# A gated decoder block on one core: features squared by partition quarters, turned in one operation, and two more feed-forward pairs by seven products

## The reference

```python
    hn = rms_norm(x, norm_mlp[l]).astype(dt)
    x = x + jnp.square(jax.nn.relu(hn @ w_up[l])) @ w_down[l]
```

## Time and profile before

| | us |
|---|---|
| median of 3 runs | 1327.31 (1327.13 to 1327.4) |
| the profiled execution | 1326.47 |
| its span, first to last instruction | 1324.7 |
| PE busy | 1320.1 |
| DVE busy | 1097.0 |
| ACT busy | 701.4 |

### The profile page before, as it was taken

One profiled execution on the slowest core, in us unless ns is written; L12 is line 12 of the kernel. 1 busy time (PEld: TensorE's weight loads), 2 busy tenths in 40 slices (PEclk: granted clock), 3 DMA queues, 4 the chain that ended last, 5 costly groups with the idle time before them and its releaser, 6 DMA issues.

```text
span 1324.7 us, 15784 instructions
## 1 busy us (share of the span) xinstructions
PE 1320.1 (100%) x5962; PEld 1095.4 (83%) x5962; DVE 1097.0 (83%) x1554; ACT 701.4 (53%) x889; POOL 16.6 (1%) x31
## 2 busy tenths in 40 slices
PE   9999999999999999999999999999999999999999
PEld 8988888888888888888888888788888888888887
DVE  6788699777477875999889998999866899899986
ACT  6656554566545444354555554555535555555553
POOL 0101000000000000000000000000000000000000
PEclk9999999999999999999999999999999999999999
DMA  9656555555556666464666665565676666556563
GB/s 319 206 177 216 195 190 179 191 181 169 186 163 203 242 215 191 166 220 162 222 190 191 192 192 190 182 213 183 216 221 189 192 191 193 191 168 211 194 218 128
DMA packets 115173, 259.57 MB, mean 196 GB/s; under 512 B 4334, under 2 KB 7452, under 8 KB 114844
## 3 DMA queue, kind: packets, MB, share of 16 engines
q1 hardware_dynamic: 115068, 258.57, 59.6%
q10 hardware_dynamic: 32, 0.01, 0.0%
HBM read 256.46 MB, written 2.10 MB: 195 GB/s over the span
## 4 chain that ended last, share of the span: by engine, by line
PE 96%; DVE 3%; issue 0%; ACT 0%; DVEq 0%; ACTq 0%
PE ps L1237 23%; PE ps L1239 23%; PE ps L1238 23%; PE ps L1247 7%; PE ps L1248 7%; PE ps L1249 7%; DVE w_lo L1109 2%; DVE ps L795 1%; PE ps L1392 1%; PE ps L1373 1%; PE ps L1341 1%; PE ps L1337 1%; PE ps L1339 1%; PE ps L1347 0%; ACT w_hi L716 0%
## 5 line engine op out<-in xcount | busy, mean ns | idle before, releaser
L477 ACT ACTIVATE w_hi<-raw 128x1024 fp32r<-128x1024 f32 (+1 forms) x349 | 368.0, 1061 | 379.7 <-PE ps L1239 363.8
L777 DVE TENSOR_TENSOR w_lo<-raw,w_hi 128x1024 fp32r<-128x1024 f32 (+1 forms) x349 | 423.9, 1222 | 166.5 <-ACT w_hi L477 163.4
L1237 PE MATMUL ps<-w_hi,xT 128*128 128x512 f32 x1088 | 425.7, 391 | 0.0
L1239 PE MATMUL ps<-w_hi,xT 128*128 128x512 f32 x1088 | 423.5, 389 | 0.0
L1238 PE MATMUL ps<-w_lo,xT 128*128 128x512 f32 x1088 | 423.3, 389 | 0.0
L1239 PEld LDWEIGHTS ps<-w_hi,xT 128*128 128x128 f32 x1088 | 204.2, 188 | 42.8
L1237 PEld LDWEIGHTS ps<-w_hi,xT 128*128 128x128 f32 x1088 | 204.3, 188 | 41.9
L1238 PEld LDWEIGHTS ps<-w_lo,xT 128*128 128x128 f32 x1088 | 204.3, 188 | 41.8
L716 ACT ACTIVATE w_hi<-raw 128x1024 fp32r<-128x1024 f32 (+1 forms) x152 | 147.7, 991 | 97.9 <-PE ps L1249 80.1
L1109 DVE TENSOR_TENSOR w_lo<-raw,w_hi 128x1024 fp32r<-128x1024 f32 (+1 forms) x152 | 167.9, 1137 | 24.3 <-ACT w_hi L716 22.4
L795 DVE STREAM_TRANSPOSE ps<-gate 32x256 f32<-32x256 f32 x272 | 124.0, 456 | 4.9
(11 more groups left out here) (242 smaller groups left out, 1360.8 us busy)
## 6 DMA issues: line engine op xcount, KB each, us to landing
raw<-in_w_in_dram SPq DMA_DIRECT2D x73, 1024.0 KB, 5.1
raw<-in_w_up_dram SPq DMA_DIRECT2D x64, 1024.0 KB, 5.3
raw<-in_w_down_dram SPq DMA_DIRECT2D x64, 1024.0 KB, 5.1
raw<-in_w_out_dram SPq DMA_DIRECT2D x16, 1024.0 KB, 5.2
raw<-in_w_branch_b_dram SPq DMA_DIRECT2D x8, 1024.0 KB, 5.3
raw<-in_w_branch_a_dram SPq DMA_DIRECT2D x8, 1024.0 KB, 5.1
raw<-in_w_in_dram SPq DMA_DIRECT2D x4, 1040.0 KB, 9.7
rows<-in_x_dram SPq DMA_DIRECT2D x1, 2048.0 KB, 9.9
```

The lines of the kernel that those rows point to most:

```text
L477: act.activation(dst[:, k % RING, :, :], src[:, k // 2, KH * (k % 2):KH * (k % 2) + KH, :], ACT.Copy).then_inc(hi_made, 1)
L777: dve.tensor_tensor(lo[:, k % RING, :, :], src[:, k // 2, KH * (k % 2):KH * (k % 2) + KH, :], hi[:, k % RING, :, :].bitcast(F32), ALU.subt ...
L1237: pe.matmul(o, hi, w_hi[:, s, i, :], start=first, stop=False)
L1239: last = pe.matmul(o, lo, w_hi[:, s, i, :], start=False, stop=end)
```

## The change

In each of the 16 up blocks ScalarE squares in 16 instructions of 32 partitions x 256 elements, four in each of the slots 1 to 4, and each writes its 32 partitions to the partition band into which it is to be turned. VectorE then turns the whole 128x1024 in one instruction in slot 5, in place of sixteen.

In the last half (f = 1, n = 1) the pairs 14 and 15 also go by seven products, which makes eight of them. The order there becomes 0, 3, 1, 5, 2, 7, 4, 9, 11, 6, 13, 8, 14, 15, 10, 12: 9 and 11, and 14 and 15, now follow directly on each other, and the last two are the whole pairs 10 and 12. For the two new pairs VectorE makes sums of features in f = 1 in slot 75 (five operations of 128x256 out of PSUM), ScalarE copies their hi part in slot 76 (128x1024), and VectorE subtracts in slot 77 (128x1024). They lie where `xT` lay, which the last up step has read by then.

```diff
-ORDER = ((0, 1, 2, 4, 6, 3, 5, 8, 7, 10, 9, 11, 12, 13, 14, 15), (0, 3, 1, 5, 2, 7, 4, 9, 6, 11, 8, 13, 10, 12, 14, 15))
-PARTS = [[4 if i in SEVEN else 2 for i in ORDER[n]] for n in range(2)]
+LATE = (14, 15)
+ORDER = (((0, 1, 2, 4, 6, 3, 5, 8, 7, 10, 9, 11, 12, 13, 14, 15), (0, 3, 1, 5, 2, 7, 4, 9, 6, 11, 8, 13, 10, 12, 14, 15)),
+         ((0, 1, 2, 4, 6, 3, 5, 8, 7, 10, 9, 11, 12, 13, 14, 15), (0, 3, 1, 5, 2, 7, 4, 9, 11, 6, 13, 8, 14, 15, 10, 12)))
+PARTS = [[[4 if i in SEVEN or f == n == 1 and i in LATE else 2 for i in ORDER[f][n]] for n in range(2)] for f in range(2)]
...
+        with nc.sbuf_tensor("late_f", [P, 4 * S], F32) as late_f, nc.sbuf_tensor("late_ops", [P, 2, 4, 2, P], F32R) as late_ops:
+            pass
         xT = sb("xT", [P, KT, 2, S], F32R)
...
# ScalarE, up_jobs
-                if j < 8 and at == 1:
-                    act.wait_ge(up_read, 8 * f + j + 1)
-                    act.activation(up_sq, up_pos, ACT.Square).then_inc(up_squared, 1)
+                if j < 8 and 1 <= at < 5:
+                    if at == 1:
+                        act.wait_ge(up_read, 8 * f + j + 1)
+                    r = P // 4 * (at - 1)
+                    read = up_pos.rearrange("p (m t q c) -> p q m t c", m=M, t=4, q=4)
+                    moved = up_sq.rearrange("p (m q t c) -> p q m t c", m=M, t=4, q=4)
+                    for q in range(4):
+                        last = act.activation(moved[32 * q:32 * q + 32, r // 32, :, :, :], read[r:r + 32, q, :, :, :],
+                                              ACT.Square)
+                    if at == 4:
+                        last.then_inc(up_squared, 1)
...
+                if f == 1 and i == 76:
+                    act.wait_ge(pair_sum, 2 * len(SEVEN) + 1)
+                    act.activation(late_parts[:, :, 0, :], late_rows, ACT.Copy).then_inc(pair_hi, 1)
...
# VectorE, up_jobs
-                if j < 8 and 2 <= at < 6:
-                    if at == 2:
-                        dve.wait_ge(up_squared, 8 * f + j + 1)
-                    turn_blocks(turned, squared, 4 * at - 8, 4 * at - 4, up_turned if at == 5 else None)
+                if j < 8 and at == 5:
+                    dve.wait_ge(up_squared, 8 * f + j + 1)
+                    dve.transpose(turned.rearrange("p (t b c) -> p b t c", t=4, c=32),
+                                  up_sq.rearrange("p (b t c) -> p b t c", t=4, c=32)).then_inc(up_turned, 1)
...
+                if f == 1 and i == 75:
+                    a11, a21, a12, a22 = (ps[:, 2 * u:2 * u + 2, P * c:P * c + P] for c in range(4))
+                    dve.wait_ge(w_used, 8 * (B_UP + FB + 8))
+                    link(dve.tensor_copy(late_4, a21))
+                    dve.tensor_tensor(late_3, a11, late_4, ALU.subtract)
+                    link(dve.tensor_tensor(late_1, late_4, a22, ALU.add))
+                    link(dve.tensor_tensor(late_2, late_1, a11, ALU.subtract))
+                    dve.tensor_tensor(late_4, a12, late_2, ALU.subtract).then_inc(pair_sum, 1)
+                if f == 1 and i == 77:
+                    dve.wait_ge(pair_hi, 2 * len(SEVEN) + 1)
+                    dve.tensor_tensor(late_parts[:, :, 1, :], late_rows, late_parts[:, :, 0, :].bitcast(F32),
+                                      ALU.subtract).then_inc(pair_lo, 1)
...
# TensorE, seven_pair
-                s1, ops = a21, sum_ops(i)
+                ops = sum_ops(i)
+                s1 = ops[:, 3, :, :] if i in LATE else a21
...
                 if first and n == 0:
                     pe.wait_ge(up_lo_made, 8 * f + 8)
+                    if f == 1:
+                        pe.wait_ge(pair_sum, 2 * len(SEVEN) + 1)
```

More of the change, by code:

```diff
@@ L155, in build @@
         e_t = gate_f[:, 0:768].rearrange("p (b c) -> p b c", b=2)
+        late_k = late_f[:, :].rearrange("p (b k c) -> p b k c", b=2, k=4)
+        late_1, late_2, late_3, late_4 = (late_k[:, :, k, :] for k in (3, 0, 1, 2))
+        late_rows = late_f[:, :].rearrange("p (r c) -> p r c", c=P)
+        late_parts = late_ops[:, :, :, :, :].rearrange("p b k a c -> p (b k) a c")
         up_pos = gate_f[:, 0:1024]
@@ L277, in step_of, with last_shared @@
         def step_of(f, n, at, part=0):
-            return 8 * (B_UP + FB * f + 8) + (sum(PARTS[0]) if n else 0) + sum(PARTS[n][:at]) + part
+            return 8 * (B_UP + FB * f + 8) + (sum(PARTS[f][0]) if n else 0) + sum(PARTS[f][n][:at]) + part
         def place_of(f, s):
-            n = 0 if s < sum(PARTS[0]) else 1
-            s -= n * sum(PARTS[0])
+            n = 0 if s < sum(PARTS[f][0]) else 1
+            s -= n * sum(PARTS[f][0])
             at = 0
-            while s >= PARTS[n][at]:
-                s -= PARTS[n][at]
+            while s >= PARTS[f][n][at]:
+                s -= PARTS[f][n][at]
                 at += 1
             return n, at, s
-        def last_shared(n):
-            return max(at for at in range(16) if PARTS[n][at] == 4)
+        def last_shared(f, n):
+            return max(at for at in range(16) if PARTS[f][n][at] == 4)
         def sum_ops(i):
+            if i in LATE:
+                return late_ops[:, LATE.index(i), :, :, :]
             q = SEVEN.index(i)
@@ L300, in diffs_before @@
         def diffs_before(f, n, at):
-            return 2 * (len(SEVEN) * (2 * f + n) + sum(x == 4 for x in PARTS[n][:at]))
+            return 2 * (len(SEVEN) * (2 * f + n) + sum(x == 4 for x in PARTS[f][n][:at]))
         def gate_kept(n):
@@ L392, in _ @@
                 for n in range(2):
-                    for at, i in enumerate(ORDER[n]):
+                    for at, i in enumerate(ORDER[f][n]):
                         k = at % RAW
@@ L1109, in down_lo @@
                 dve.tensor_tensor(lo, src, hi.bitcast(F32), ALU.subtract).then_inc(lo_made, 1)
-                if PARTS[n][at] == 4 and part == 1:
+                if PARTS[f][n][at] == 4 and part == 1:
                     quarters = raw[:, k, :, :]
@@ L1119, in first_sums @@
                 diffs = w_diff.rearrange("p (a n) -> p a n", n=N)
-                before = [step_of(f, n, x, 2) for x in range(at) if PARTS[n][x] == 4]
+                before = [step_of(f, n, x, 2) for x in range(at) if PARTS[f][n][x] == 4]
                 dve.wait_ge(landed[at % RAW], 16 * (B_UP + 16 * f + 8 + 4 * n + at // RAW) + 16)
@@ L1203, in _ @@
                 blk0 = B_UP + FB * f
-                for i in range(12, 64 + DOWN + (12 if f == 0 else 0)):
+                for i in range(12, 64 + DOWN[f] + (12 if f == 0 else 0)):
                     up_jobs(f, i)
@@ L1207, in _ @@
                         split_lo(blk0 + i // 8, i % 8)
-                    elif i < 64 + DOWN:
+                    elif i < 64 + DOWN[f]:
                         n, at, part = place_of(f, i - 64)
-                        if part == PARTS[n][at] - 1 and at < 15 and PARTS[n][at + 1] == 4:
+                        if part == PARTS[f][n][at] - 1 and at < 15 and PARTS[f][n][at + 1] == 4:
                             first_sums(f, n, at + 1)
@@ L1213, in _ @@
                     else:
-                        split_lo(blk0 + FB + (i - 64 - DOWN) // 8, i % 8)
+                        split_lo(blk0 + FB + (i - 64 - DOWN[f]) // 8, i % 8)
                     for n in range(2):
-                        end = step_of(f, n, last_shared(n), 3)
+                        end = step_of(f, n, last_shared(f, n), 3)
                         if 8 * blk0 + i in (end + 3, end + 4):
@@ L1255, in whole_pair @@
             def whole_pair(f, n, at):
[L1257 removed]
+                i = ORDER[f][n][at]
                 for part in range(2):
@@ L1282, in seven_pair @@
             def seven_pair(f, n, at):
-                i = ORDER[n][at]
+                i = ORDER[f][n][at]
                 own, shared = OWN[n], SHARED[n]
-                first, end = PARTS[n][:at].count(4) == 0, at == last_shared(n)
+                first, end = PARTS[f][n][:at].count(4) == 0, at == last_shared(f, n)
                 a11, a21, a12, a22 = (feature(2 * i + t, m) for t in range(2) for m in range(M))
-                s1, ops = a21, sum_ops(i)
+                ops = sum_ops(i)
+                s1 = ops[:, 3, :, :] if i in LATE else a21
                 s2, s3, s4 = (ops[:, c, :, :] for c in range(3))
```

35 lines of the change are left out of this document (18 added, 17 removed).

## The result

| | before | changed |
|---|---|---|
| median of 9 runs, us | 1327.13 (1326.61 to 1327.4) | 1331.02 (1329.49 to 1331.67) |
| the profiled execution | 1326.47 | 1331.6 |
| its span | 1324.7 | 1329.8 |

The changed kernel is slower: ratio 1.0031, 95% interval 1.0022 to 1.0039. I had forecast 1328.0, within 1325.4 to 1330.4; 1331.02 lies outside, and on the side to which I had given 0.13.

The account below looks back on a forecast made before the run. TensorE, busy 1320.1 of 1324.7 us, was taken as the bound. Terms -0.74 + 1.4 - 1.24 + 0.57 + 0.75 = +0.7 us gave 1328.0 against the median of 1327.31, range 1325.4 to 1330.4.

Parts of the forecast that it names:

- Durations and counts: Squares near 0.41 us, turn near 1.25; VectorE some 97 us less busy, ScalarE 66 more, 6 matmuls fewer.
- the up blocks: Blocks 0 to 6: added ScalarE and saved VectorE work change nothing on TensorE's path; no gaps there.
- the join of f=0: Block 7 into the down part, f=0: VectorE is 2.4 us earlier, TensorE's gap at 842 goes, -0.74 us.
- The pace of the squares: Slots 1 to 4: ScalarE's squares overlap by 0.09, 0.32 us apiece, 2.25 a slot with the split.
- The upper bound in the text: Squares at 0.48 without overlap: 2.9 us a slot, hi of step 72 2.0 us late, all paid at f=1's join.
- a forecast +1.4: Join of block 7 and down part, f=1: late sums on VectorE's chain make TensorE's gap 1.7 us, not 0.3.
- the sign of being wrong: Wrong if TensorE has gaps in the up blocks, or the gap at 1184 is below 1 or above 2.5 us.
- The room for the squares: Block 7: a slot's 2.25 us is under TensorE's 2.72, so hi of step 72 still comes at 1167.60.
- The matmuls: Last half: two whole pairs become pairs by seven products, 6 matmuls fewer, -1.24 us.
- The neighbours: Last half: 9 and 11, and 14 and 15, as neighbours cost 0.29 us each, +0.57 together.
- The end: Before the last pair: TensorE waits for lo parts behind add_shared's first half, +0.75 us, bounds 0.3 and 1.1.
- ScalarE becomes the bound: Rival, slots 1 to 4: decides at 0.44 us a square; at 0.6, 1333.5. Chance 0.13 with a dear turn.

Follow-up runs that it names:

- experiment 1: Changed kernel's squares by quarters and single turn, with the six pairs and order of the kernel before, no late sums: 1325.95 us, ratio 0.9993 to before.
- experiment 10: Changed kernel with only two of the four squares per slot in block 7 of f=1: 1327.7 us, ratio 1.0006 to the kernel before.
- experiment 7: Kernel before with three added 128x1024 subtractions on VectorE ahead of the last split of pair 3 in f=1: 1332.81 us, ratio 1.0039.
- experiment 8: Kernel before with one added 128x1024 subtraction on VectorE ahead of the last split of pair 3 in f=1: 1327.92 us, ratio 1.0007.
- experiment 9: Changed kernel with late sums made later and only pair 14 added, seven pairs in another order: 1325.6 us, ratio 0.999 to the kernel before.
- experiment 2: Changed kernel's eight pairs, order and late sums, with the one square and sixteen turns of the kernel before: 1331.48 us, ratio 1.0038 to before.
- experiment 5: Changed kernel with late work moved off the join, three neighbourhoods and three whole pairs at the end: 1327.24 us, ratio 1.0003 to the kernel before.
- experiment 11: Changed kernel with late sums made later and both halves of add_shared behind the last split: 1325.9 us, ratio 0.9993 to the kernel before.
- experiment 4: Changed kernel with the late sums and their hi and lo parts all moved off the join of f=1: 1326.29 us, ratio 0.9996 to the kernel before.
- experiment 3: Changed kernel with only the late hi and lo parts moved, into pair 11 by mistake, sums left in slot 75: 1328.56 us, ratio 1.0014 to before.
- experiment 12: Changed kernel with only both halves of add_shared moved behind the last split: 1330.75 us, ratio 1.0026 to the kernel before.

## Why the prediction was wrong, step by step

- **Durations and counts, the up blocks, the join of f=0**: right. The squares are 0.414, the turn 1.254 us, no gap in the up blocks, and -0.74 at the join of f=0 (its gap is absent in the changed kernel and in experiment 1). VectorE's 82 us for a forecast 97 left out the new sums and what two more pairs by seven cost it; by the prediction's own numbers that is about 3.2 + 2 x (6.6 - 2.3) = 12 us, an estimate. ScalarE's 95 us for a forecast 66 come mostly from the overlap that was not there: 256 squares at 0.41 and not 0.32, and a late copy of 1 us.
- **The pace of the squares: the step that failed.** I took 0.09 us of overlap for each instruction from two copies in the earlier trace rows and set 0.32 apiece, 2.25 us a slot. Measured: 0.42 apiece, 2.79 a slot, so hi of step 72 slips by 1.5 us. The upper bound in the text (2.0 us late) held it, but the value was taken from the wrong neighbour, and the term came out at +2.9 (3.33 - 0.40) for a forecast +1.4. The gap of 2.76 us is over the 2.5 that the prediction had named as the sign of being wrong. Experiment 10 shows that ScalarE's lateness is the whole difference in the gap: without it the gap is 1.71 for 1.7. The Trainium skill has the right warning (VectorE: DVE Perf Modes, the section on the TRN2 errata): small tiles pay the fixed latency for each instruction. I had weighed it as load, where it acted as lateness. By another page of the Trainium skill (Vector Engine (DVE) Microarchitecture Reference, section 5.2), ScalarE takes 0.833 ns a column and about 98 ns an instruction; an estimate from that is 0.31 us for 256 columns, and these instructions, at 0.42, don't agree.
- **The room for the squares: the test was wrong too.** "2.25 < 2.72" asks for the rhythm of a slot, but the four slots of block 7 have 9.52 us, 2.38 each, as 1158.08 and 1167.60 in the earlier trace rows say. Counted as it counts its upper bound, 1159.05 + 16 squares + 3 x 0.97, hi of step 72 comes late from 0.35 us apiece on. The line's 0.41, taken without the overlap, would already have given 0.9 us.
- **The clock behind a gap: a term that was missing.** I priced a gap at its own length. This one cost 1.6 us more in the profiled run, and experiments 7 and 8 show that the gap alone can do it, though not in every run.
- **The matmuls**, 6 fewer: right, and experiment 9 gains with three of them. **The neighbours**: 9 and 11 cost 0.54 in the changed kernel's trace, and 0.29 in those of experiments 2 and 10; 14 and 15 cost 0.34. Forecast 0.29 each. Where the 0.54 stands, a split of ScalarE at 1270.50 began 0.3 us later than in the usual cycle; why is open.
- **The end**: 0.87 us, forecast 0.75, by the mechanism named (experiments 5 and 11 remove it). What I did not see in experiment 11 is that the additions moved behind the last split are then late at the outputs.
- **The sum** by the trace: -0.74 + 2.93 + 1.57 - 1.24 + 0.54 + 0.34 + 0.87 = +4.3 us; the medians say +3.9, the two spans +5.1. Some 0.9 of the spans' difference is there when the down part of f=0 begins (811.44 and 812.32), ahead of every gap in this sum; its cause is open.
- **The rivals**: "ScalarE becomes the bound" was in kind the true one. Its deciding point, 0.44 us apiece, was set by the slot of 2.72 us; by the room that there was it is 0.35, and the squares are at 0.42. I gave it 0.13. A point of decision that lies 0.03 us from the value I took (0.32), and below the line's 0.41, is no ground for that.

## What to carry to other kernels

When work is put on an engine just where a second engine is already late, price it by the chain (who is late, who then waits), not by load: 3.2 us of VectorE's work cost next to nothing where it waited anyway, and some 4.4 us more than that at this join (experiment 4 against the changed kernel). Count the room of an engine from the instruction it really starts behind, not from the rhythm of the steady stretch. Ask what a gap of TensorE brings behind it: here one of 2.8 us cost from nothing to nearly 2 us more, one of 3.5 us from nothing to some 3. And an overlap seen between two instructions is that pair's; for a new shape take the full duration until a trace shows otherwise.

## What the runs showed of the hardware

- ScalarE's squares of 32x256 that move data between bands of partitions start 0.42 us apart at a duration of 0.414. A split of 128x1024 in front of them takes 0.96 us in slot 1, where the first square leaves partitions 0 to 31 in their place, and 1.08 in the slots 2 to 4, where it reads other partitions and moves them. In experiment 10 it is 1.09 in slots 3 and 4 too, where ScalarE had been idle before the split. Copies of 128x128 and 128x384 overlapped by 0.09. Whether the 32 partitions, the shift or the access pattern does it was not tried.
- One turn of 128x1024 lasts 1.25 us, as long as 1024 elements should by the line through turns of 32 partitions: the four bands go side by side.
- After 2.8 us (profiles of the changed kernel and experiment 2) and 3.5 us (that of experiment 7) without a matmul TensorE's granted clock was at 1.2 GHz for about 3 us. After 1.2, 1.3 and 1.7 us (experiments 8, 3 and 10) it stayed at 2.4 GHz, and after 2.8 us in the profile of experiment 12 as well.
- The same kernel does both. By the mean granted clock of each run it fell in eight of nine runs of the changed kernel, six of ten of experiment 12 and four of five of experiment 7. A run in which it did not took less time: 1.5 us under the median of the changed kernel, 1.9 between the middles of the two groups of experiment 12 (1329.1 and 1331.0), 3.2 under the median of experiment 7.
